# Rotary queries and keys of the differential part: from token-major to feature-major

## The reference

```
qkv = h @ w_qkv                                  # h: 512 x 1024 normed, w_qkv: 1024 x 3072
q, k = ... reshape(b, s, 8 heads, 2, 64)
rope:  x1, x2 = first 8, next 8 of the 64 features of a half head
       [x1 * cos - x2 * sin, x2 * cos + x1 * sin], the other 48 stay
sc = einsum('bqhcd,bkhcd->bhcqk', q, k) * 64 ** -0.5
a = softmax(sc[0]) - lam * softmax(sc[1]);  o = a @ v;  rms_norm(o);  o @ w_o
```

## Time and profile before

| | |
|---|---|
| median of 3 runs | 1744.97 us (1744.77 to 1745.62) |
| profiled execution | 1745.7 us |
| its span, first to last instruction | 1743.9 us |
| mean granted TensorE clock | 0.998 of full |
| instructions | 22594 |

### The profile page before, as it was taken

One profiled execution on the slowest core, in us unless ns is written; L12 is line 12 of the kernel. 1 busy time (PEld: TensorE's weight loads), 2 busy tenths in 40 slices (PEclk: granted clock), 3 DMA queues, 4 the chain that ended last, 5 costly groups with the idle time before them and its releaser, 6 DMA issues.

```text
span 1743.9 us, 22594 instructions
## 1 busy us (share of the span) xinstructions
PE 1728.2 (99%) x8782; PEld 1460.0 (84%) x8782; DVE 1091.1 (63%) x1719; ACT 785.4 (45%) x1398; POOL 134.5 (8%) x138
## 2 busy tenths in 40 slices
PE   9999999999999999999999999999999999999998
PEld 7888888888888888888888888889898888888887
DVE  5788644344346666685864764665888676376375
ACT  5553532222235555544532432456876454244244
POOL 2003200000005100002000000022101200000000
PEclk9999999999999999999999999999999999999999
DMA  5212333333333221122333333323111233333341
GB/s 169 73 51 85 93 97 97 97 97 97 97 97 97 78 69 61 61 73 85 96 97 97 97 93 101 97 76 103 39 49 37 81 92 98 98 98 97 98 127 61
DMA packets 128355, 152.78 MB, mean 88 GB/s; under 512 B 9286, under 2 KB 101992, under 8 KB 128248
## 3 DMA queue, kind: packets, MB, share of 16 engines
q1 hardware_dynamic: 128088, 151.26, 28.3%
q10 hardware_dynamic: 160, 0.07, 0.0%
HBM read 148.61 MB, written 2.10 MB: 86 GB/s over the span
## 4 chain that ended last, share of the span: by engine, by line
PE 94%; DVE 3%; ACT 1%; issue 1%; DMA 1%; POOL 0%; ACTq 0%; DVEq 0%; POOLq 0%
PE bk L1908 24%; PE bk L1909 23%; PE bk L1910 23%; PE bk L1937 5%; PE bk L1939 4%; PE bk L1938 4%; PE bk L1913 4%; PE bk L2035 2%; PE bk L2069 1%; PE bk L2068 1%; PE bk L1996 1%; PE bk L2023 1%; DVE WL L2100 1%; PE bk L2025 0%; PE bk L2024 0%
## 5 line engine op out<-in xcount | busy, mean ns | idle before, releaser
L1908 PE MATMUL bk<-R,WH 128*128 128x512 f32 x1844 | 724.0, 393 | 1.8 <-DVE R L2106 1.6
L1910 PE MATMUL bk<-R,WL 128*128 128x512 f32 x1844 | 718.4, 390 | 0.0
L1909 PE MATMUL bk<-R,WH 128*128 128x512 f32 x1844 | 718.1, 389 | 0.0
L2100 DVE TENSOR_TENSOR WL<-RAW,WH 128x1024 fp32r<-128x1024 f32 (+4 forms) x278 | 343.7, 1237 | 483.2 <-ACT WH L2302 482.2
L2302 ACT ACTIVATE WH<-RAW 128x1024 fp32r<-128x1024 f32 (+4 forms) x278 | 288.0, 1036 | 604.3 <-PE bk L1910 546.6
L1908 PEld LDWEIGHTS bk<-R,WH 128*128 128x128 f32 x1844 | 346.8, 188 | 73.4 <-issue 2.2
L1910 PEld LDWEIGHTS bk<-R,WL 128*128 128x128 f32 x1844 | 346.4, 188 | 72.8
L1909 PEld LDWEIGHTS bk<-R,WH 128*128 128x128 f32 x1844 | 346.8, 188 | 68.9
L1937 PE MATMUL bk<-WH,R 128*128 128x256 f32 (+4 forms) x432 | 146.0, 338 | 0.3 <-DVE KT L2106 0.3
L1939 PE MATMUL bk<-WL,R 128*128 128x256 f32 (+4 forms) x432 | 140.7, 326 | 0.0
L1938 PE MATMUL bk<-WH,R 128*128 128x256 f32 (+4 forms) x432 | 140.5, 325 | 0.0
(11 more groups left out here) (170 smaller groups left out, 1503.6 us busy)
## 6 DMA issues: line engine op xcount, KB each, us to landing
RAW<-in_ffn_w_up_dram SPq DMA_DIRECT2D x176, 256.0 KB, 3.0
RAW<-in_ffn_w_down_dram SPq DMA_DIRECT2D x44, 512.0 KB, 3.7
RAW<-in_w_gate_dram SPq DMA_DIRECT2D x44, 256.0 KB, 2.8
RAW<-in_w_up_dram SPq DMA_DIRECT2D x44, 256.0 KB, 3.1
RAW<-in_w_down_dram SPq DMA_DIRECT2D x22, 512.0 KB, 3.7
RAW<-in_da_w_qkv_dram SPq DMA_DIRECT2D x32, 256.0 KB, 2.9
RAW<-in_w_out_dram SPq DMA_DIRECT2D x8, 512.0 KB, 3.6
RAW<-in_da_w_qkv_dram SPq DMA_DIRECT2D x8, 512.0 KB, 3.6
```

Source lines behind the costliest of these rows:

```text
L1908: e.matmul(dst, lh, rh, start=start, stop=False)
L1909: e.matmul(dst, lh, rl, start=False, stop=False)
L1910: return e.matmul(dst, ll, rh, start=False, stop=stop)
L2100: e.tensor_tensor(low, sides(st.n, RAW[:, r, 0:m]), high.bitcast(F32), ALU.subtract).then_inc(on["wlo_dve"], 1)
```

## The change

The query and key product of the differential part becomes feature-major: four banks, two tiles of queries and two of keys, each 128 features by 512 tokens. There is no TOK buffer, no GpSimd step and no transpose for it. `ev_rotated` has VectorE do it all: `rot_swap` exchanges the rows of features 0 to 7 and 8 to 15 of each 64 while it reads the bank, `scaled` multiplies the bank by a table of cosines, `rot_sine` multiplies the swapped rows by a table of signed sines, `rot_add` adds. The tables (1 and 0 where a feature isn't rotary) come from DRAM (`rot_load`, 128 x 1024) and are multiplied once by the norm's factor (`rot_spread`), which an `over` of its own spreads. The two buffers TOK hold the tables and eight tiles: three swapped, five out. The factor 1/8 goes into the split of the queries. Steps of the MLA part that reuse TOK wait for the low halves of all four groups instead of one.

```diff
@@ class Norm, total
-                    st = yield step("both_out", dst=r.r, eighth=r.r8, r=o, r2=o2, after=[rooted2])
+                    st = yield step("both_out", dst=r.r, r=o, r2=o2, after=[rooted2])
@@ build
+        rot.out, rot.swapped = Ring(5), Ring(3)
...
+        def rotation(N):
+            for x in rot.out.fr:
+                x.free = list(tok_free)
+            emit("rot_load", after=[])
+            landing(s_rot, free_at["pe"] + 20000.0)
+            while N() is None or N().rooted is None:
+                yield None
+            b = yield from bank()
+            st = yield step("over", bank=b.i, r=N().r, after=counts([b.free, N().rooted]))
+            st = yield step("rot_spread", bank=b.i, after=counts([st.pe, (s_rot, 16)]))
+            put_bank(b, st.dve)
+            rot.spread = st.dve
@@ qkv_group
-            def ev_qk(t, bk, done):
...
-            def turn_in():
...
-            def turn_q(n):
...
-            def turn_k(n):
...
+            def ev_rotated(m, bk, done):
+                while rot.spread is None or m < 2 and G.Q[m].h is None:
+                    yield None
+                z, o = (yield from taken_from(rot.swapped)), (yield from taken_from(rot.out))
+                st = yield step("rot_swap", dst=rot.at(z), bank=bk.i, after=counts([done, z.free]))
+                swapped = st.dve
+                st = yield step("scaled", dst=rot.at(o), bank=bk.i, bc=rot.cos, after=counts([done, o.free, rot.spread]))
+                turned = st.dve
+                put_bank(bk, swapped, turned)
+                st = yield step("rot_sine", z=rot.at(z), after=[swapped, rot.spread])
+                st = yield step("rot_add", z=rot.at(z), o=rot.at(o), after=[st.dve, turned])
+                rot.swapped.put(z, st.dve)
+                if m < 2:
+                    lo = yield from split_pair(G.Q[m], rot.at(o), [st.dve], 0.125)
+                else:
+                    while before and not before.valued:
+                        yield None
+                    i = G.kbase + 4 * (m - 2)
+                    lo = yield from halves(KT[:, i, :], KT[:, i + 1, :], rot.at(o), [st.dve], None, [kfree[i + x] for x in range(4)])
+                    kready[i] = [lo]
+                rot.out.put(o, lo)
+                G.ups.append(lo)
...
-                spawn(turn_in())
-                yield from gemm_t(N.X, 8, 512, ev_qk)
+            yield from gemm_f(N.X, 8, 4, ev_turned if kind == "fg" else ev_rotated)
@@ ev_lat
-                                after=counts([done, Gs[2].ups, NM.rooted]))
+                                after=counts([done, [G.ups for G in Gs], NM.rooted]))
@@ kpe
-            masked = yield step("mask_key", after=[])
+            masked = yield step("mask_key", after=toks)
@@ products
+            last.n = None
+            spawn(rotation(lambda: last.n))
             yield from ffn(N2, value_plain, da_norm)
@@ vector_program
+                    e.tensor_tensor(rot.cos, BK[st.bank][:, :], rot.cos, ALU.mult).then_inc(on["rot_spread_dve"], 1)
+                    e.tensor_tensor(rot.sin, BK[st.bank][:, :], rot.sin, ALU.mult).then_inc(on["rot_spread_dve"], 1)
...
+                    e.stream_shuffle(st.dst, BK[st.bank][:, :], [x ^ 8 if x < 16 else x for x in range(32)]).then_inc(on["rot_swap_dve"], 1)
...
+                    e.tensor_tensor(st.z, st.z, rot.sin, ALU.mult).then_inc(on["rot_sine_dve"], 1)
...
+                    e.tensor_tensor(st.o, st.o, st.z, ALU.add).then_inc(on["rot_add_dve"], 1)
```

More of the change, by code:

```diff
@@ L691, in total @@
                     r.r = r.r1 = o
[L692 to L695, removed]
                     r.rooted = rooted
@@ L865, in put @@
                 lo = yield from split_pair(Q[n], bank[0:rows, :], [done], rows=slice(0, rows))
[L866 to L874, removed]
                 return [lo]
@@ L1211, in in_line, with taken_from @@
                 spawn(fill_by(t, pairs), 0)
+        rot = Group()
+        rot.spread, rot.cos, rot.sin = None, flat(1)[:, 0:S], flat(1)[:, S:2 * S]
+        rot.out, rot.swapped = Ring(5), Ring(3)
+        for x in rot.swapped.fr:
+            x.i += 5
+        rot.at = lambda x: flat(0)[:, x.i * S:x.i * S + S] if x.i < 5 else flat(1)[:, (x.i - 3) * S:(x.i - 2) * S]
+        def taken_from(ring):
+            while not ring.fr:
+                yield None
+            return ring.get()
+        def rotation(N):
[10 more added lines that the diff above has]
+            rot.spread = st.dve
         def qkv_group(G, g, N, kind, spent, prior=None, before=None):
@@ L1589, in ev_q @@
             def ev_q(t, bk, done):
-                used = Gs[3].ups if g == 0 else lat.ups if g == 1 else before.qups
+                used = [x for G in Gs for x in G.ups] if g == 0 else lat.ups if g == 1 else before.qups
                 while lat.rooted is None or len(used) < (6 if g == 1 else 4):
@@ L1872, in sync_program @@
                     load(st.n)
+                elif st.kind == "rot_load":
+                    e.dma_start(flat(1)[:, 0:2 * S], a["rot"]).then_inc(s_rot, 16)
                 elif st.kind == "tri_load":
@@ L2137, in vector_program @@
                     times_add(st.o, st.c, 1.5, st.y, ALU.add, ALU.mult).then_inc(on["root_out_dve"], 1)
-                elif k == "eighth":
-                    for done in st.after:
-                        w.wait_ge(*done)
-                    e.tensor_scalar(st.dst, st.src, 0.125, None, ALU.mult).then_inc(on["eighth_dve"], 1)
                 elif k == "both_in":
@@ L2348, in scalar_program @@
                     e.activation(st.dst, BK[st.bank][:, :], ACT.Copy).then_inc(on["over_copy_act"], 1)
-                elif k == "tok_qk":
-                    for done in st.after:
-                        w.wait_ge(*done)
-                    e.activation(TOKS[st.tok][:, st.t, 0:256], BK[st.bank][:, 0:256], ACT.Copy, scale=st.rq)
-                    e.activation(TOKS[st.tok][:, st.t, 256:512], BK[st.bank][:, 256:512], ACT.Copy, scale=st.rk).then_inc(on["tok_qk_act"], 1)
                 elif k == "tok_q":
@@ L2457, in gpsimd_program @@
                 elif k == "mask_key":
+                    for done in st.after:
+                        w.wait_ge(*done)
                     src = CN[:, C_MK:C_MK + 16].rearrange("p (t c) -> p t c", c=4)
```

72 lines of the change are left out of this document (40 added, 32 removed).

## The result

The changed kernel takes 1762.86 us, the median of four runs (1760.38 to 1763.8), beside 1745.1 us for the kernel before on the same chip: a ratio of 1.0097, with a 95% interval of 1.0084 to 1.011. It is 1% slower, where 0.7% was forecast. The profiled execution took 1762.69 us, its span is 1760.8 us and the mean granted clock 0.994.

What follows compares the result with a forecast made beforehand. TensorE, busy 99%, was taken as the bound. From the profiled 1745.7 us, less 7.5 of work, plus waits of 9.9 (first group) and 10.1 (later groups), gave 1758.2; less 0.7 for the median, 1757.5 us, range 1749 to 1763.

Steps and rivals of the forecast that it cites:

- What goes from TensorE: Differential part: transposes save 7.0 us, feature-major steps 0.9, the extra `over` costs 0.4; net 7.5 us less work.
- VectorE's passes and order: Rotation: four passes a bank at 0.60 us each, settle before swap, about 3.1 us from bank to bank.
- Rival (d): Rotation: the shuffle takes 1.23 us, each bank comes 0.6 us later, time near 1767 us; chance 0.12 together with Rival (c).
- The wait for banks in the first group: First group's value product: TensorE waits for banks held until swap and cosine, behind settle; 9.9 us.
- The value product follows at once and its first step needs one of them back: After the query and key product fills four banks, the value product must wait for one; 5.6 us in the first group.
- later groups: Value products of groups two to four: waits for banks of 4.1, 3.0 and 3.0 us, together 10.1 us.
- In the tail nothing changes: End of the differential part: TensorE's work is whole and keys come no later against the product; 0 us.
- Rival (c): Behind the first group's wait, matmuls run at 1.2 GHz, costing 4.5 us; 1762 us; chance 0.12 together with Rival (d).
- (a): Differential part: the removed work goes and nothing waits, banks come back in time; 1737.5 us; chance 0.25.
- (b): Differential part: only part waits, 5 to 10 us in all; 1742 to 1748 us; chance 0.15.

Runs made afterwards that it cites:

- e5: Changed kernel with the sine multiply and the add left out, so the output lacks the sine part; 1743.94 us.
- e4: Kernel before, with four VectorE row maxima over 512 columns of constants added to each of 16 TOK evictions, results unused, no bank held; 1759.59 us.
- e9: Changed kernel with only the sine multiply left out, three added VectorE passes a bank; 1751.0 us.
- e10: Changed kernel with the product split, queries' half before keys' half, settle in its place and all four passes on VectorE; 1782.4 us.
- e1: Changed kernel without swap, sine multiply and add, the cosine multiply kept, so the output lacks the rotary part; 1743.64 us.
- e12: Changed kernel with the product split into queries' and keys' halves and settle ranked behind the rotation, all four passes on VectorE; 1761.03 us.
- e8: Changed kernel with the product split into queries' and keys' halves, settle ranked behind the rotation and the sine multiply on GpSimd; 1746.29 us.
- e2: Changed kernel with the eight settle steps (residual times norm factor) ranked behind the rotation; 1756.09 us.
- e6: Kernel before, with eight additions of 128x512 on GpSimd added per group, for which nobody waits; 1750.15 us.

## Why the prediction came out as it did

Sign and size were right (1757.5 forecast, 1762.86 measured, inside the range), in part by luck: the largest wait of the forecast never came, and waits elsewhere and lost clock stood in for it.

**What goes from TensorE: forecast 7.5 us, measured 5.5.** In e5, where the clock was 1.00 throughout the stage, it lasted from 566.29 to 820.41, less 4.8 of idle: 249.4 us of work. Before it was 255.8 - 0.9 = 254.9. Of the 2 us missing, 0.9 is a misreading: 18 steps of either product, switch included, take 4.20 us before (571.93 to 576.13) and 4.18 us after (573.08 to 577.26), so feature-major gains nothing; the difference in the earlier trace rows was between a stretch without switches and one with them. The rest, 1.1 us, isn't resolved.

**VectorE's passes and order: right.** The shuffle's mean is 736 ns, the multiplies' 683. Cosine passes ended at 582.4, 584.8, 587.9 and 590.9, where 581.9, 584.3, 587.4 and 590.5 were forecast; the stage itself began 0.7 us later than before. Rival (d) falls. The Trainium skill (VectorE: DVE Perf Modes, section "The perf-mode tier table (the rule you actually need)") has the shuffle about level with the multiply, and the trace agrees: 8% apart.

**The wait for banks in the first group, 9.9 us: the step that failed.** "The value product follows at once and its first step needs one of them back" is wrong. The cap of four says when a step may be *placed*; the bank that it then gets is the one that has been free longest of all eight. By the planned order these are four banks last used by the residual, the norm and the tables' `over`, free before 575 us, so 96 matmuls ran without a gap. That reading of the cap comes from the code; the trace shows the missing gap. In later groups such waits exist, 3.3 us in all, where 10.1 were forecast.

**What took its place.** The rotation's 16 passes a group delay what stands behind them on VectorE, and most of what is waited for there are again banks, only others than the forecast ones: those of the values' low halves (1.9 and 1.2 us in the first group), of the transposed probabilities' low halves (1.8, 1.6) and of the heads' outputs (1.9), 8.4 us beside the 3.3 of the rotation's own. The prediction had the kind of wait right and looked at one product's banks alone. That these are waits for banks is read from the code, the planned order and the times in the trace; no run gives those steps a free bank. e4 shows without the change that the queue is enough: load that nobody waits for, and 12 us of idle. Waits of 14.5 us more in all, against 20.0 forecast.

**"In the tail nothing changes": wrong.** The prediction took the window of 750 to 760 us for the tail. The last chain (output, norm, product) comes later, and in it TensorE waited for 0.9 us even before. After, it stands open with 1.42 and 2.26 us of wait at 805 and 808 us and half the clock behind them. VectorE isn't behindhand there; less product work is left to put beside the chain. That attention has slipped against the products and so left less is the likely reason; no run isolates it.

**Rival (c), waits cost clock: right in kind, in other places.** It put 4.5 us behind the first group's wait, which didn't come, so its 1762 us is near the measured time by luck too. The clock cost about 8 us, from 597, 730 and 808 us on: 272.5 us of stage less 15.4 of idle less 249.4 of work at full clock leaves 7.7 us, and the windows give 8.5. So the books read -5.5 + 14.5 + 7.7 = +16.7 us. The forecast was -7.5 + 20.0 = +12.5. The same sum, idle plus clock less 0.9, less 5.5 where the product is feature-major, is within about 2 us of the profiled execution's time less before's median for ten of the twelve other kernels; e9 (3.0 us off) and e10 (4.1) are the exceptions.

**Rivals (a) and (b)** are met only where VectorE gets less: e1 and e5 don't reach 1737.5 either, since 2 us of work were never to be had and 2 to 5 us wait or run slow even then.

What stays open: which property of the planned order makes e10 and e12, the same work but for settle's rank, differ by 21 us. The experiments show that it does, not how to foresee it. No kernel that computes everything was faster than the one before; e8 comes within 0.2% of it.

## What to carry to other kernels

An engine that is 63% busy on average can still be the one that everybody waits for: price added work there by what stands *behind* it in its queue, and by every bank that those later passes read and give back, not only by the buffers that the new work holds. A limit on how many buffers a product may have isn't yet a wait: look at which buffer is handed out and when that one came free. Where an order is fixed by a planner, measure several placements of the same work before judging a change; here four with all passes on VectorE (after, e2, e10, e12) lay between 1756.1 and 1782.4 us, 26 us apart, more than the change itself.

## What the hardware showed unasked

GpSimd's passes slow VectorE's work on SBUF, 128x4 columns from 162 to 274 ns on average, in a kernel where neither of the two waits for the other (e6). Passes that read a bank weren't slowed: two low halves from PSUM took 1.29 us beside eight GpSimd passes, and 1.29 us in the kernel before.

```profile
583.67 10.71 POOL L2458 TENSOR_TENSOR FS<-CN 128x512 f32<-128x512 f32 x8
586.18 1.29 DVE L2113 TENSOR_TENSOR R<-bk,R 128x512 fp32r<-128x512 f32 x2
...
633.58 1.00 DVE L2097 SCALAR_TENSOR_TENSOR SM<-SM 128x4 f32<-128x4 f32 x1
```

TensorE's clock fell to 1.2 GHz behind two idle stretches of 1.42 and 2.26 us in the tail, and stood there from 807.94 to 812.7 us. In the changed kernel's second group, idle of 0.18 and 1.36 us at 629 and 632 us left the clock at full level, so not every short gap costs. Behind a wait of 1.64 us at 747.7 us the steps took 0.43 us again. What tells these apart wasn't tried.
